# Value products with the values as the stationary operand, two heads into the two partition halves, reciprocals of the totals turned in place of the output

## The reference

```python
# group A: sliding window over two chunks of 64 keys, learned sink per head
logits = einsum('bnqgrd,bnkgd->bngrqk', qc, kb) * HEAD_DIM ** -0.5 - slopes * dist
m = maximum(max(logits, -1), sink)
p = exp(logits - m);  denom = sum(p, -1) + exp(sink - m)
out_a = einsum('bngrqk,bnkgd->bnqgrd', p / denom, vb)
# group B: an indexer scores all visible keys, each query keeps 256 of them
_, idx = lax.top_k(score, 256)
probs = softmax(where(sel_valid, q @ kg * HEAD_DIM ** -0.5 - slopes * dist, -inf))
out_b = einsum('bhqk,bqkd->bqhd', probs, vg)     # one key and value head for all 8
mix = concatenate([out_a, out_b], -1) @ w_o
```

## Time and profile before

| | us |
|---|---|
| median of 3 runs (3342.18 to 3348.17) | 3345.27 |
| the profiled execution | 3335.3 |
| its span, first to last instruction | 3333.5 |
| TensorE busy, matmul records | 2954.4 (89%) |
| weight loads busy | 2409.7 (72%) |
| VectorE busy | 1686.7 (51%) |
| ScalarE busy | 1574.6 (47%) |
| GpSimd busy | 314.9 (9%) |
| mean granted TensorE clock | 0.918 |

### The profile page before, as it was taken

One profiled execution on the slowest core, in us unless ns is written; L12 is line 12 of the kernel. 1 busy time (PEld: TensorE's weight loads), 2 busy tenths in 40 slices (PEclk: granted clock), 3 DMA queues, 4 the chain that ended last, 5 costly groups with the idle time before them and its releaser, 6 DMA issues. The chain is left out here.

```text
span 3333.5 us, 42857 instructions
## 1 busy us (share of the span) xinstructions
PE 2954.4 (89%) x14649; PEld 2409.7 (72%) x14649; DVE 1686.7 (51%) x3080; ACT 1574.6 (47%) x3023; POOL 314.9 (9%) x990
## 2 busy tenths in 40 slices
PE   6678888887887787899897999999999999999997
PEld 2456666666666676788786788788878887888876
DVE  2125667686886878955454444244422543244422
ACT  1336877878787686885432222232223222232222
POOL 0001322212121121120011000000000000000000
PEclk8678888888988888888998999999999999999999
DMA  5110000000000000110555333343333433343323
GB/s 212 45 48 29 29 20 22 15 13 4 14 14 14 10 4 7 39 55 17 168 176 168 97 95 99 114 142 98 94 108 119 127 101 88 120 145 94 96 93 107
DMA packets 316075, 254.86 MB, mean 76 GB/s; under 512 B 9153, under 2 KB 271905, under 8 KB 315809
## 3 DMA queue, kind: packets, MB, share of 16 engines
q1 hardware_dynamic: 282544, 236.29, 22.8%
q10 hardware_dynamic: 33392, 16.81, 1.8%
HBM read 219.50 MB, written 33.57 MB: 76 GB/s over the span
## 5 line engine op out<-in xcount | busy, mean ns | idle before, releaser
L1964 ACT ACTIVATE p_hi<-raw 128x1024 fp32r<-128x1024 f32 x264 | 279.3, 1058 | 692.1 <-PE dbank L1935 353.0
L2038 DVE TENSOR_TENSOR p_lo<-raw,p_hi 128x1024 fp32r<-128x1024 f32 x264 | 323.4, 1225 | 423.8 <-ACT p_hi L1964 423.6
L1288 DVE TENSOR_SCALAR_CACHE_REDUCE above<-score,cand 128x384 uint8<-128x384 f32 (+6 forms) x224 | 315.8, 1410 | 4.3
L1135 ACT ACTIVATE signs<-score,pick 128x512 int8<-128x512 f32 (+6 forms) x224 | 304.4, 1359 | 25.7 <-POOL pick L631 17.0
L1113 ACT ACTIVATE logit<-tbank 128x512 f32<-128x512 f32 (+3 forms) x448 | 214.7, 488 | 204.9 <-PE tbank L849 202.2
L1916 PE MATMUL gbank<-x_hi,p_hi 128*128 128x512 f32 x704 | 275.3, 391 | 29.2 <-DVE p_lo L2038 29.2
L865 PE MATMUL obank<-vb,logit 128*128 128x64 f32 x2176 | 300.2, 283 | 0.0
L849 PE MATMUL tbank<-ident,logit 128*128 128x128 f32 x1336 | 251.0, 301 | 51.2 <-ACT logit L1103 48.7
L865 PEld LDWEIGHTS obank<-vb,logit 128*128 128x128 f32 x2176 | 294.0, 208 | 0.0
L1933 PE MATMUL dbank<-p_hi,a_hi 128*128 128x512 f32 x704 | 277.6, 394 | 17.0 <-DVE a_lo L2066 14.1
L731 PE MATMUL work<-w_in,h_T 128*128 128x512 f32 (+1 forms) x768 | 283.2, 516 | 0.7 <-ACT h_T L929 0.7
(11 more groups left out here) (219 smaller groups left out, 5250.2 us busy)
## 6 DMA issues: line engine op xcount, KB each, us to landing
raw<-in_w_gate_up SPq DMA_DIRECT2D x176, 512.0 KB, 3.8
raw<-in_w_down SPq DMA_DIRECT2D x88, 512.0 KB, 3.7
ada<-in_w_ada ACTq DMA_DIRECT2D x32, 512.0 KB, 3.9
wada<-in_w_ada SPq DMA_DIRECT2D x4, 2048.0 KB, 15.6
x_in<-in_x SPq DMA_DIRECT2D x16, 512.0 KB, 3.9
mixT<-oT SPq DMA_DIRECT2D x32, 256.0 KB, 2.4
mix<-mixT SPq DMA_DIRECT2D x16, 512.0 KB, 6.2
x_rows<-in_x SPq DMA_DIRECT2D x16, 512.0 KB, 4.6
```

The source lines that it names most:

```text
L1135: nc.scalar.activation(signs[:, 0:L], score[:, b % 2, 0:L], ACT.Sign, scale=-1.0, bias=pick[:].bitcast(F32), accum_out=less_more[:]).then_ ...
L1288: link(nc.vector.tensor_scalar(above[:, 0:L], score[:, b % 2, 0:L], cand[:].bitcast(F32), None, ALU.is_ge, ALU.add, accum_out=count[:]), b ...
L1964: nc.scalar.activation(p_hi[:, s], raw[:, s], ACT.Copy).then_inc(panel_high, 1)
L2038: nc.vector.tensor_tensor(p_lo[:, s], raw[:, s], p_hi[:, s].bitcast(F32), ALU.subtract).then_inc(panel_ready, 1)
```

## The change

The value products swap their operands. The values [128 keys x 64] are loaded as weights and the turned probabilities [128 keys x 128 queries] move; the result is [64 channels x 128 queries], already turned. Two neighbouring heads, i (even) and i+1, are issued in turn for each key tile: head i into partitions 0 to 63, head i+1 into 64 to 127 of the same columns of `obank`. The number of products and of records stays the same. For a pair of heads i and i+1, all groups but the last are issued in slot i+3 (group c-1 behind the transposes of group c), the last one in slot i+4, behind the first piece and ahead of the transposes. `pv_done` counts pairs' groups.

The totals now lie along queries on partitions while the output lies along channels. `invert_totals` on VectorE (slot i+2) makes the reciprocals, spreads each over 64 columns into `rtotal_wide` (which is the memory of `oT`), TensorE turns that (`turn_totals`, slot i+3, in a group number of its own of `tbank`), ScalarE copies it to `rtotal_T`, and VectorE's `scale_output` multiplies `obank` by it straight into `oT`. `turn_output`, `copy_output` and `o_norm` go.

```diff
@@ Plan.__init__
-            t += -(-len(key_tiles(kind, b)) // 4)
+            t += -(-len(key_tiles(kind, b)) // 4) + (h == HEADS - 1)
+    def values_done(self, i):
+        pairs = self.heads[0:i // 2 * 2 + 1:2]
+        return sum(-(-len(key_tiles(kind, b)) // 4) for kind, b, _ in pairs)
+    def turned_totals(self, i):
+        return self.group0[i + 1] - 1
@@ TensorE
+            def turn_totals(i):
+                kind, b, h = plan.heads[i]
+                t = plan.turned_totals(i)
+                pe.wait_ge(rtotal_ready, OUT_ORDER.index((kind, b)) + 1)
+                if t >= 2:
+                    pe.wait_ge(pt_ready, t - 1)
+                for j in range(4):
+                    mm = nc.tensor.transpose(tbank[t % 2][:, j * P:(j + 1) * P], rtotal_wide[:, j, :], ident[:])
+                mm.then_inc(pt_full, 1)
             def weighted_values(i, g):
-                pe.wait_ge(pt_ready, t + 1)
+                pe.wait_ge(pt_ready, plan.group0[i + 1] + g + 1)
                 for j, kt in enumerate(tiles):
-                    v = vb[:, kt, :] if kind == "B" else va[:, kt % 4, HD * (h // 4):HD * (h // 4 + 1)]
-                    mm = nc.tensor.matmul(obank[o % 2][:, h * HD:(h + 1) * HD], 
-                                          logit[:, i % 4, (4 * g + j) * P:(4 * g + j + 1) * P], v,
-                                          start=(g == 0 and j == 0), stop=(last and j == len(tiles) - 1))
+                    for r in range(2):
+                        v = vb[:, kt, :] if kind == "B" else va[:, kt % 4, HD * (h // 4):HD * (h // 4 + 1)]
+                        mm = nc.tensor.matmul(obank[o % 2][r * HD:(r + 1) * HD, h // 2 * P:(h // 2 + 1) * P], v,
+                                              logit[:, (i + r) % 4, (4 * g + j) * P:(4 * g + j + 1) * P],
+                                              start=(g == 0 and j == 0), stop=(last and j == len(tiles) - 1))
                 mm.then_inc(pv_done, 1)
             def head(i):
-                values = len(plan.groups(i - 3)) if 3 <= i < n + 3 else 0
-                for c in range(max(pieces, groups, values)):
+                pair = i - 3 if i % 2 else i - 4
+                values = len(plan.groups(pair)) if 0 <= pair < n else 0
+                for c in range(max(pieces, groups, 1)):
                     if c < pieces:
                         piece(i, c)
+                    if c == 0 and i % 2 == 0 and values:
+                        weighted_values(pair, values - 1)
+                    if c == 0 and 3 <= i < n + 3 and plan.heads[i - 3][2] == HEADS - 1:
+                        turn_totals(i - 3)
                     if c < groups:
                         transpose_group(i - 2, c)
-                    if c < values:
-                        weighted_values(i - 3, c)
-                if 5 <= i < n + 5:
-                    turn_output(i - 5)
+                    if i % 2 and 1 <= c < values:
+                        weighted_values(pair, c - 1)
@@ ScalarE, at the head of slot i+3 of a block's eighth head
-                nc.scalar.activation(oT[:], pairs(obank[o % 2][:]), ACT.Copy).then_inc(o_copied, 1)
+                act.wait_ge(pt_full, t + 1)
+                if o:
+                    act.wait_ge(o_made, o)
+                nc.scalar.activation(rtotal_T[:], pairs(tbank[t % 2][:]), ACT.Copy).then_inc(pt_ready, 1)
@@ VectorE
             def logits(i, c):
                 if c == 0 and i >= 4:
-                    dve.wait_ge(pv_done, plan.group0[i - 3])
+                    dve.wait_ge(pv_done, plan.values_done(i - 4))
+            def invert_totals(i):
+                dve.wait_ge(exp_done, i + 1)
+...
+                if o:
+                    dve.wait_ge(o_stored, 16 * o)
+                nc.vector.tensor_copy(rtotal_wide.rearrange("p j (r d) -> p (j r) d", d=HD),
+                                      rtotal[:].unsqueeze(2).to_broadcast([P, HEADS, HD])
+                                      ).then_inc(rtotal_ready, 1)
             def scale_output(i):
...
+                dve.wait_ge(pv_done, plan.values_done(i))
+                dve.wait_ge(pt_ready, plan.turned_totals(i) + 1)
+                nc.vector.tensor_tensor(oT[:], obank[o % 2][:].rearrange("p (j t) -> p j t", t=P), rtotal_T[:],
+                                        ALU.mult).then_inc(o_made, 1)
```

More of the change, by code:

```diff
@@ L484, in mixing @@
         rtotal = sb("rtotal", [P, HEADS])
-        o_norm = sb("o_norm", [P, HEADS, HD])
+        rtotal_T = sb("rtotal_T", [P, 4, P])
         oT = sb("oT", [P, 4, P])
@@ L491, in mixing @@
         mod_bias, mod_gain, mod_add = (ada[0:MOD_STEPS, i, :] for i in range(3))
+        rtotal_wide = oT[:]
         squares = h_T[:].rearrange("p k t -> p (k t)")
@@ L536, in mixing @@
         pick_counted = sem("pick_counted")
-        o_scaled = sem("o_scaled")
-        o_turned = sem("o_turned")
-        o_copied = sem("o_copied")
+        rtotal_ready = sem("rtotal_ready")
+        o_made = sem("o_made")
         o_stored = sem("o_stored")
@@ L567, in _ @@
                     load_x(b + 2)
[L569 removed]
+                sp.wait_ge(o_made, i + 1)
                 row0 = 0 if kind == "A" else HEADS * HD
@@ L855, in weighted_values @@
                 last = g == len(plan.groups(i)) - 1
-                t = plan.group0[i] + g
-                pe.wait_ge(pt_ready, t + 1)
+                pe.wait_ge(pt_ready, plan.group0[i + 1] + g + 1)
                 o = OUT_ORDER.index((kind, b))
                 if g == 0 and h == 0 and o >= 2:
-                    pe.wait_ge(o_copied, o - 1)
+                    pe.wait_ge(o_made, o - 1)
                 for j, kt in enumerate(tiles):
-                    v = vb[:, kt, :] if kind == "B" else va[:, kt % 4, HD * (h // 4):HD * (h // 4 + 1)]
-                    mm = nc.tensor.matmul(obank[o % 2][:, h * HD:(h + 1) * HD],
-                                          logit[:, i % 4, (4 * g + j) * P:(4 * g + j + 1) * P], v,
-                                          start=(g == 0 and j == 0), stop=(last and j == len(tiles) - 1))
-                mm.then_inc(pv_done, 1)
-            def turn_output(i):
-                kind, b, h = plan.heads[i]
-                if h < HEADS - 1:
-                    return
-                o = OUT_ORDER.index((kind, b))
-                pe.wait_ge(o_scaled, o + 1)
-                for j in range(4):
-                    mm = nc.tensor.transpose(obank[o % 2][:, j * P:(j + 1) * P],
-                                             o_norm[:, 2 * j:2 * j + 2, :].rearrange("p h d -> p (h d)"), ident[:])
-                mm.then_inc(o_turned, 1)
+                    for r in range(2):
[3 more added lines that the diff above has]
+                                              start=(g == 0 and j == 0), stop=(last and j == len(tiles) - 1))
+                mm.then_inc(pv_done, 1)
             def head(i):
@@ L921, in _ @@
                     i += 1
-            for j in range(5):
+            for j in range(3):
                 head(i + j)
@@ L1141, in head @@
                 waiting = list(actions)
-                if 6 <= i < n + 6:
-                    copy_output(i - 6)
+                if 3 <= i < n + 3 and plan.heads[i - 3][2] == HEADS - 1:
+                    copy_totals(i - 3)
                 for g in range(max(groups, 1)):
@@ L1178, in _ @@
                     i += 1
-            for j in range(6):
+            for j in range(3):
                 head(i + j)
@@ L1353, in logits @@
                                                accum_out=into).then_inc(piece_read, 1)
+            def invert_totals(i):
+                kind, b, h = plan.heads[i]
+                if h < HEADS - 1:
+                    return
+                o = OUT_ORDER.index((kind, b))
+                dve.wait_ge(exp_done, i + 1)
+                sums = total[:, o % 2, :]
+                if kind == "A":
+                    link(nc.vector.tensor_tensor(sums, sums, exp_sink[:, o % 2, :], ALU.add))
+                link(nc.vector.reciprocal(rtotal[:], sums))
+                if o:
[3 more added lines that the diff above has]
+                                      ).then_inc(rtotal_ready, 1)
             def scale_output(i):
@@ L1377, in own_work @@
                         logits(i, part)
-                    elif i >= 4:
-                        scale_output(i - 4)
+                    else:
+                        if i >= 2:
+                            invert_totals(i - 2)
+                        if i >= 4:
+                            scale_output(i - 4)
             def head(i, kind, b, h, actions):
@@ L1444, in _ @@
             for j in range(4):
+                if j < 2:
+                    invert_totals(i + j - 2)
                 scale_output(i + j - 4)
```

22 lines of the change are left out of this document (4 added, 18 removed).

## The result

| | before | after |
|---|---|---|
| median of 4 runs (range) | 3346.17 (3342.18 to 3348.17) | 3369.57 (3369.00 to 3370.99) |
| the profiled execution | 3335.3 | 3369.0 |
| mean granted TensorE clock | 0.918 | 0.914 |
| last store of `mixing` issued | 1606.5 | 1638.3 |

What follows compares the result with a forecast made beforehand. TensorE was taken as first limit everywhere, a second engine close below in the middle. 3335.3 - 77 + 32 + 9 + 3 - 1.4 gave about 3301 us profiled, 3311 median; own range 3275 to 3335, 8 in 10 3240 to 3378.

Steps and rivals of the forecast that it cites:

- The overlap: Value products in different column halves run side by side on TensorE: 0.060 us a record, saving 160 us of TensorE time.
- Rival A: No overlap of value products, each record still 0.112 us, bunching costs more: about 3380 us; chance 0.20.
- So I take a switch at nothing.: Entering and leaving the narrow tile on TensorE costs no time, judged from one transpose with 32 columns.
- The step's own upper bound, 67 us: Most that tile switches could cost TensorE: 448 switches at 0.15 us each.
- C: Rival: each tile switch costs 0.15 us, 67 us of TensorE time, 33 us at the end: 3344 us; chance 0.08.
- The pass-on: Share of TensorE's saving reaching the end: 77 of 160 us; 0.4 between 311 and 1365 us, 0.85 in the last stretch.
- the last stretch: From 1494 to 1605 us TensorE stands alone, so 0.85 of 26 us saved there reaches the end: 22 us.
- The totals' chain, at 11 us: Totals in place of outputs: 9 us for VectorE's spread copy, 3 us for waits, -1.4 us at the end of `mixing`.
- The 1.4 us at the end of `mixing`: Gain between last value record and store's issue, 2.30 us before, where one product of 0.69 and its hand-over stay.
- Part 2: Issuing by pairs adds waits: 19 us for VectorE (128 x 0.5 x 0.3), 13 for TensorE on ScalarE's copies; 32 us in all.
- B: Rival: the ring eats the overlap; middle pass-on 0.15, waits double, over 30 us on copies or `obank`: 3370 us; chance 0.10.
- D: Rival: a less busy TensorE is granted a lower clock, 0.83 in place of 0.87 in the middle: 3331 us; chance 0.10.

Runs made afterwards that it cites:

- experiment 4: Changed kernel with value products one head at a time in the old kernel's order, narrow tile entered 448 times, no overlap: 3436.76 us, ratio 1.0256.
- 10: experiment 4 with 128 columns of values as weights, so no narrow product is left: 3373.48 us, ratio 1.0081.
- experiment 9: Kernel before with the value products of only the first half of each group's tiles, 1264 records fewer: 3305.24 us, ratio 0.9873.
- 13: experiment 4 with a head's key tiles going into the two halves by turns, so products overlap within one head: 3384.60 us, ratio 1.0124.
- 3: Changed kernel with head i's products of a group all ahead of head i+1's: 3394.82 us, ratio 1.0138.
- 14: 10 without the totals' chain, output multiplied by ones: 3308.72 us, ratio 0.9891.
- 1: Changed kernel without the totals' chain (no spreading, turn or copy; output multiplied by ones): 3334.22 us, ratio 0.9956.
- 11: Changed kernel without VectorE's spread copy, each reciprocal column read 64 times as a narrow stationary operand: 3383.29 us, ratio 1.0111.
- 12: 7 without VectorE's spread copy, the same edit as in 11: 3367.42 us, ratio 1.0058.
- 5: Changed kernel with the totals turned and copied at the end of slot i+3 instead of its head: 3370.21 us, ratio 1.0061.
- 7: 6 with the totals turned and copied at the end of the slot, as in 5: 3362.93 us, ratio 1.0045.
- 6: Changed kernel with a deeper circular store for the probabilities and value groups one step later: 3380.72 us, ratio 1.0096.
- 15: Complete version: full-width weights padded with zeros, before's order, circular store, totals' chain one slot later; against before: 3344.98 us, ratio 0.9996.
- experiment 2: Kernel before with only the value products' order changed to pairs of heads, old operands and output: 3456.06 us, ratio 1.0309.

## Why the prediction was wrong

The forecast was 3311 with a range of its own of 3275 to 3335. The 3369.6 us lie outside it, and inside the 3240 to 3378 that were to hold 8 in 10.

**The overlap, right.** 0.060 us a record was forecast and 0.0545 measured; 2672 x (0.1115 - 0.0545) = 152 us at the high clock. Rival A is refuted. The Trainium skill, page "TensorEngine Tiling (Array Packing)", section "Overview", has up to 2x; 0.1115 / 0.0545 is 2.05 inside a group, and 0.109 / 0.0545 is 2.0 against a narrow record alone in its half (experiment 4).

**The step that failed first: "So I take a switch at nothing."** It rested on the earlier trace rows, one transpose with 32 columns and no gap around it, and on calling that the same case. Experiments 4 and 10 put 0.26 to 0.32 us on each way in and out. The kernel after goes in 224 times (64 A pairs and 160 groups of B pairs), which makes 224 x (0.26 to 0.32) = 58 to 72 us of TensorE time. The sum agrees roughly: 152 - 73 = 79 us of the saved work did not appear in it (67 by the other limit). Half of the 59 us between 4 and 10, for half the entries, is an estimate of 29 us of time, about as much as the whole loss. The step's own upper bound, 67 us, was the right size. What stood in C's place as a sign, a gap of 0.1 to 0.2 us ahead of the first record and behind the last, is there.

**The pass-on, too high.** 77 of 160 us, 0.48, were to reach the end. Experiments 9 and 13 give 0.30 and 0.32. By stretch, the traces of experiment 9 and before (one execution each, 33 us apart up to the store) show: between 311 and 1365 us 864 records less, 97 us at the high clock, and 15.5 us of time, 0.16 where 0.4 was taken; from the end of ScalarE's last search round (1494.0 us before, 1475.7 in 9) on 216 records less, 24 us, and 14.3 us of time (98.2 against 112.5), 0.59 where 0.85 was taken. Each us less on TensorE mostly became idle time on it: 293 us before, 368 in experiment 9, 394 after. In the kernel after the last stretch, where 22 us were to come, gave 1 to 3: from the end of the search to the store 109.2 us after 112.5, and the last exponent as late as the one at 1497 us. Work that is added isn't passed on whole either: 118 us of narrow-tile cost put 59 us on the end (4 against 10, 0.5), and 52 us put 22 on it (3 against after, 0.42).

**The totals' chain, at 11 us (9 + 3 - 1.4) over the old output path.** In the old order it costs 27 over that path (10 against before) and 64 in all (10 against 14). In the order by pairs it costs 35 to 39 in all (after against 1); what the old path would cost there no run measured, so how much of the 11 was wrong in the kernel after stays open. Its instructions are as cheap as was said, the copy cheaper (0.43 us, not 0.69), and taking that copy away doesn't help (11, 12). The size is in the waits. Moving it within the slot gives nothing with the ring of four places (5) and 17 us with the deeper store (7 against 6); a whole slot more, with the deeper store, brought 28 us (15 against 10). The 1.4 us at the end of `mixing` didn't come: from the end of the last value record to the store 2.0 us pass after 2.3, since VectorE waits there for the turned totals.

**Part 2, at 32 us, about right or high.** Its two waits came as described: VectorE's on `obank` 111.3 us, more than the 64 of its sum before the share uncovered, while its waits for logits fell by 94, and TensorE's on ScalarE's copy 60.5 on the loads. Taking VectorE's away gives nothing alone (6) and 7 to 9 us with late totals (7 against after). The loss can be walked through in single steps: before to 10, +27 (totals in place of outputs); 10 to 4, +59 (448 narrow entries); 4 to 13, -44 (overlap); 13 to after, -17; together the +24. The last step holds the order by pairs and 224 entries less. With the estimate of 29 us for those, the order is left with some 12. That is a remainder, not a measurement, and the prices don't simply add: from full width in the old order to the kernel after's narrow pairs it is -3 us with the chain (after against 10) and +22 without it (1 against 14).

**The rivals.** B forecast 3370 and the time is 3369.6, with its sign (waits over 30 us) in the trace. It isn't the cause as it was put: with its wait on VectorE gone, most of the loss stays, and it had the switch at nothing. Its lower pass-on in the middle, 0.15, was the part that held (0.16 in experiment 9). That its sum hits the time to 1 us is luck, since it leaves out the switch and the chain. C had the mechanism and, with 0.15 us a switch or 0.30 for in and out, the size; it said 3344, since it kept the rest of the forecast. D: the granted clock is 0.914 after 0.918, the low clock costs 169 us and not 166: nothing.

**Still open:** why the order by pairs with the old operands (2) draws a lower clock, and the kernels at full width head by head (10, 14, 15) a higher one, and how far the chain's price depends on that; and which link of the chain holds the ring in after, since each that was moved alone gave nothing.

## What to carry to other kernels

Price a change of tile shape by how often it happens, from an instruction of the same kind with the same width and not from a transpose that looks alike; with short groups between full-width work the entries ate about half of what the overlap gave here. Where three engines pass work around a ring of few places, count a saving on the busiest at a third until a run of the kernel with that work left out says otherwise, lower where a second engine is nearly as full and higher where it stands alone; an addition cost 0.4 to 0.5 of itself here. A sum of waits isn't a price: a wait that was taken away came back under another name (experiments 5 and 6). A step that goes over three engines costs its waits more than its instructions, and slack for it pays only where the ring around it has slack too.

## What was not expected of the hardware

- Two float32 products in different halves of the columns start 6 to 7 ns apart, and two take 0.109 us where one alone takes as long (0.109 with 64 columns of weights, 0.111 with 128).
- Going into products with 64 columns of weights and out of them costs 0.26 to 0.32 us of TensorE together, seen as 0.17 us of idle time on each side that no engine's event releases; one transpose with 32 columns had shown none.
- The two halves needn't alternate record by record to overlap: issued four and four, 8 records took 0.056 us each; issued eight and eight, the second half's began beside the first half's fifth, and 16 records took 1.51 us and not 1.95.
- The granted clock differs by kernel with nearly the same products: a mean of 0.897 in experiment 2, 0.918 before, 0.931 in 15 and 0.935 in 14.
